# Final norms of a one-core backbone step: one VectorE pass is given to ScalarE and GpSimd, and loads are moved ahead of the last scatter

## The reference

```python
def layer_norm(x, g, b):
    mu = jnp.mean(x, axis=-1, keepdims=True)
    var = jnp.mean(jnp.square(x - mu), axis=-1, keepdims=True)
    return (x - mu) * lax.rsqrt(var + LN_EPS) * g + b
x = layer_norm(DEEPNORM_ALPHA * x1 + g2 * moe(h, p), ln2_g, ln2_b)
```

## Time and profile before

| | us |
|---|---|
| median of three runs | 1805.2 |
| lowest and highest | 1798.62, 1807.9 |
| the profiled execution | 1803.54 |
| its span, first to last instruction | 1801.5 |
| TensorE busy | 1689.4 (94%) |
| VectorE busy | 931.5 (52%) |
| ScalarE busy | 847.2 (47%) |
| GpSimd busy | 768.4 (43%) |

### The profile page before, as it was taken

How to read it: one execution, slowest core, us unless ns; L and a number is a source line. 1 busy time by engine, 2 the same in 40 slices (tenths; PEclk the granted TensorE clock), 3 DMA queues, 4 the chain that set the end, 5 groups by cost and what they waited for, 6 DMA issues and landing times.

```text
span 1801.5 us, 32620 instructions
## 1 busy us (share of the span) xinstructions
PE 1689.4 (94%) x8585; PEld 1319.0 (73%) x8586; DVE 931.5 (52%) x1453; ACT 847.2 (47%) x950; POOL 768.4 (43%) x445
## 2 busy tenths in 40 slices
PE   6999999999899898999999999999999999999944
PEld 2677778888455586888888788788888887878821
DVE  7532311158478883444546465554554655555528
ACT  2321012262032442546667666665756666767612
POOL 2230000400003564437556656566556565665620
PEclk9999999999999898999999999999999999999968
DMA  8515531021552363668978888888879888988776
GB/s 349 176 50 175 176 118 38 24 97 41 216 200 81 118 223 131 239 181 263 307 242 302 293 271 279 281 290 293 266 244 296 265 277 288 284 297 274 231 243 259
DMA packets 102448, 390.77 MB, mean 217 GB/s; under 512 B 21668, under 2 KB 38305, under 8 KB 74625
## 3 DMA queue, kind: packets, MB, share of 16 engines
q1 hardware_dynamic: 62576, 289.25, 43.4%
q0 software_dynamic: 37232, 91.44, 20.0%
q10 hardware_dynamic: 2592, 9.44, 1.7%
HBM read 339.94 MB, written 84.72 MB: 236 GB/s over the span
## 4 chain that ended last, share of the span: by engine, by line
PE 75%; DMA 8%; DVE 7%; ACT 3%; issue 3%; POOL 2%; ACTq 1%; SPq 1%; DVEq 0%; POOLq 0%
PE ps L874 42%; PE ps L2037 12%; PE ps L929 5%; DMA arena<-hx_dram,arena 4%; PE ps L2178 4%; PE ps L1960 2%; PE ps L906 1%; POOL d_split L612 1%; DMA acc_dram<-arena 1%; PE ps L2168 1%; PE ps L2010 1%; DMA arena<-ada_halves 1%; PE ps L1906 1%; PE ps L2072 1%; ACT const L697 1%
## 5 line engine op out<-in xcount | busy, mean ns | idle before, releaser
L874 PE MATMUL ps<-gu_split,xT 128*128 (+1 forms) x2712 | 635.8, 390 | 0.0
L874 PEld LDWEIGHTS ps<-gu_split,xT 128*128 128x128 f32 x2712 | 508.8, 188 | 107.5 <-issue 2.3
L612 POOL TENSOR_TENSOR d_split<-raw,d_split (+1 forms) x65 | 299.7, 4610 | 160.3 <-ACT d_split L676 159.6
L874 PE MATMUL ps<-d_split,hTe 128*128 (+1 forms) x1356 | 345.4, 404 | 15.6 <-ACT arena L752 14.2
L1010 DVE TENSOR_TENSOR gu_split<-raw,gu_split (+1 forms) x130 | 293.5, 2299 | 98.0 <-ACT gu_split L671 98.0
L874 PEld LDWEIGHTS ps<-d_split,hTe 128*128 128x128 f32 x1356 | 250.1, 191 | 69.4 <-issue 19.2
L671 ACT ACTIVATE gu_split<-raw (+1 forms) x130 | 241.9, 1909 | 27.8 <-SPq L510 19.6
L640 POOL DMA_INDIRECT acc_dram<-arena x104 | 168.9, 1624 | 131.2 <-DVE arena L1185 109.0
L631 POOL DMA_INDIRECT arena<-hx_dram,arena x108 | 147.8, 1368 | 143.4 <-DVE arena L1180 114.4
L1174 DVE TENSOR_TENSOR arena<-ps,arena 128x256 f32<-128x256 f32 x113 | 70.3, 622 | 259.0 <-ACT arena L758 258.9
L1164 DVE TENSOR_TENSOR xT<-ps,xT 128x1024 fp32r<-128x1024 f32 x115 | 140.7, 1224 | 107.0 <-ACT xT L730 107.0
(11 more groups left out here) (303 smaller groups left out, 1430.3 us busy)
## 6 DMA issues: line engine op xcount, KB each, us to landing
raw<-w_exp_gate SPq DMA_DIRECT2D x64, 1024.0 KB, 7.1
raw<-w_exp_up SPq DMA_DIRECT2D x64, 1024.0 KB, 11.1
raw<-w_exp_down SPq DMA_DIRECT2D x64, 1024.0 KB, 7.7
arena<-w_ada SPq DMA_DIRECT2D x16, 1024.0 KB, 5.0
arena<-x_dram SPq DMA_DIRECT2D x18, 512.0 KB, 10.7
arena<-acc_dram SPq DMA_DIRECT2D x18, 512.0 KB, 11.3
arena<-ada_halves SPq DMA_DIRECT2D x4, 2048.0 KB, 24.6
w_raw<-w_in SPq DMA_DIRECT2D x16, 512.0 KB, 5.0
```

The lines of the kernel that those rows point to most:

```text
L612: tt(d_split(q, 1), raw_d(q), d_split(q, 0).bitcast(F32), ALU.subtract).then_inc(d_low, 1)
L874: last = mm(dst, lhs(a, j), rhs(b, j), start=(t == 0), stop=(t == len(terms) - 1))
```

## The change

VectorE's fourth pass (L1302) is kept for tile 8 alone. For tiles 0 to 7 VectorE only makes the reciprocal; ScalarE multiplies `acc1_t[i]` in place by it (a Copy with a scale per partition), after the Square and Sqrt of the next tile, and GpSimd adds `ln2_b` and writes `acc_t[i]`. SyncE writes tiles out in order as before, tile 8 after tile 7.

The loads are regrouped. x1 of tiles 3 to 8 is loaded as soon as all experts are split. GpSimd now waits for accumulator 1 first and signals, then for accumulator 0, and signals again; after the first signal `g2_row[1]` and all nine tiles of accumulator 1 are loaded, after the second the nine tiles of accumulator 0. GpSimd also waits, before either, for a count of `xT_ready` that says that the buffer `xT`, which `acc1_t` overlaps, is written no more. Three semaphores of the routing tables (`end_mm`, `cmp_ready`, `blk_mm`) are folded into `rank_mm` and `nb_ready`; those waits stand where they stood.

```diff
@@ SyncE
             sp.wait_ge(gu_low, NE)
             sp.wait_ge(d_low, NE)
+            for i in range(XE, NT):
+                sp.dma_start(x1_t[i], x1_dram[tile(i), :]).then_inc(fin_in[i], 16)
             sp.wait_ge(moe_done, 1)
+            sp.dma_start(g2_row[1], mod_dram[1, 3 * D:4 * D].partition_broadcast(P)).then_inc(fin_in[ST], 16)
+            for i in range(NT):
+                sp.dma_start(acc1_t[:, i, :], acc_dram[1][tile(i), :]).then_inc(fin_in[i], 16)
+            sp.wait_ge(moe_done, 2)
             for i in range(NT):
                 sp.dma_start(acc_t[:, i, :], acc_dram[0][tile(i), :]).then_inc(fin_in[i], 16)
-                sp.dma_start(acc1_t[:, i, :], acc_dram[1][tile(i), :]).then_inc(fin_in[i], 16)
-                if i >= XE:
-                    sp.dma_start(x1_t[i], x1_dram[tile(i), :]).then_inc(fin_in[i], 16)
-            sp.dma_start(g2_row[1], mod_dram[1, 3 * D:4 * D].partition_broadcast(P)).then_inc(fin_in[ST], 16)
             for i in range(NT):
-                sp.wait_ge(fin_ready, i + 1)
+                if i < NT - 1:
+                    sp.wait_ge(fin_ready, i + 1)
+                else:
+                    sp.wait_ge(last_ready, 1)
@@ GpSimd, after the last scatter
-            for p in range(2):
+            pool.wait_ge(xT_ready, NT + last + 4)
+            for p in (1, 0):
                 pool.wait_ge(y_out[p], 8 * last + 32)
-            pool.nop().then_inc(moe_done, 1)
+                pool.nop().then_inc(moe_done, 1)
+            pool.wait_ge(row_ready, 16 * (8 + 3))
+            for i in range(NT - 1):
+                pool.wait_ge(scaled, i + 1)
+                tt(acc_t[:, i, :], acc1_t[:, i, :], ln2_row[:, 1, :], ALU.add).then_inc(fin_ready, 1)
@@ ScalarE
             for i in range(NT):
                 ln_std(2 * NT + i, acc_t[:, i, :])
+                if i:
+                    r = i - 1
+                    act.wait_ge(scale_ready, r + 1)
+                    a(acc1_t[:, r, :], acc1_t[:, r, :], ACT.Copy, scale=lrec[:, r % 2:r % 2 + 1]).then_inc(scaled, 1)
@@ VectorE
                 i = s - 1
-                if i >= 0:
+                if 0 <= i < NT - 1:
+                    r = i % 2
+                    dve.wait_ge(std_ready, 2 * NT + i + 1)
+                    if i >= 2:
+                        dve.wait_ge(scaled, i - 1)
+                    dve.reciprocal(lrec[:, r:r + 1], lstd[:, r:r + 1]).then_inc(scale_ready, 1)
+                elif i == NT - 1:
+                    dve.wait_ge(scaled, NT - 2)
                     scale = ln_scale(2 * NT + i)
-                    stt(acc_t[:, i, :], acc1_t[:, i, :], scale, ln2_row[:, 1, :], ALU.mult, ALU.add).then_inc(fin_ready, 1)
+                    stt(acc_t[:, i, :], acc1_t[:, i, :], scale, ln2_row[:, 1, :], ALU.mult, ALU.add).then_inc(last_ready, 1)
@@ TensorE and VectorE, routing tables
-                    mm(ps[0:1, 7, 0:1], cnt, ones[0:E, :], start=True, stop=True).then_inc(end_mm, 1)
+                    mm(ps[0:1, 7, 0:1], cnt, ones[0:E, :], start=True, stop=True).then_inc(rank_mm, 1)
-                    dve.wait_ge(end_mm, 1)
+                    dve.wait_ge(rank_mm, 7)
...
```

More of the change, by code:

```diff
@@ L419, in build @@
         x0r_in, x1_out, h2_out = (x0r_in0, x0r_in1), (x1_out0, x1_out1), (h2_out0, h2_out1)
-        (sel_ready, rank_mm, nb_ready, end_mm, cmp_ready, blk_mm, tables_ready, dest_ready, empty_out, perm_ready) = (sem(n) for n in (
-             "sel_ready", "rank_mm", "nb_ready", "end_mm", "cmp_ready", "blk_mm", "tables_ready", "dest_ready",
+        (sel_ready, rank_mm, nb_ready, tables_ready, scale_ready, scaled, last_ready, dest_ready, empty_out, perm_ready) = (sem(n) for n in (
+             "sel_ready", "rank_mm", "nb_ready", "tables_ready", "scale_ready", "scaled", "last_ready", "dest_ready",
              "empty_out", "perm_ready"))
@@ L979, in phase3_pe @@
                     mm(ps[0:1, 7, 5 * E:6 * E], C["tokid"][0:E, 0:1], at_pos[:, 0:E], start=True, stop=True)
-                    mm(ps[0:1, 7, 0:1], cnt, ones[0:E, :], start=True, stop=True).then_inc(end_mm, 1)
+                    mm(ps[0:1, 7, 0:1], cnt, ones[0:E, :], start=True, stop=True).then_inc(rank_mm, 1)
                 if b == 6:
-                    pe.wait_ge(cmp_ready, 1)
+                    pe.wait_ge(nb_ready, 2)
                     mm(ps[:, 7, 0:1], cmp_b[:, 0:P], skip, start=True, stop=True)
                     mm(ps[0:NBP - P, 7, 1:2], cmp_b[:, P:NBP], skip, start=True, stop=True)
-                    mm(ps[0:1, 7, 4 * E:4 * E + NBP], ones[0:E, :], cmp_b, start=True, stop=True).then_inc(blk_mm, 1)
+                    mm(ps[0:1, 7, 4 * E:4 * E + NBP], ones[0:E, :], cmp_b, start=True, stop=True).then_inc(rank_mm, 1)
             last = routed_steps(pe, step)
@@ L1264, in phase3_dve @@
                     done(dve.tensor_copy(endc, ps[0:E, 7, 7 * E + 1:7 * E + 2]))
-                    ts(cmp_b, C["blk"][0:E], endc, None, ALU.is_ge).then_inc(cmp_ready, 1)
+                    ts(cmp_b, C["blk"][0:E], endc, None, ALU.is_ge).then_inc(nb_ready, 1)
                 if b == 6:
-                    dve.wait_ge(blk_mm, 1)
+                    dve.wait_ge(rank_mm, 8)
                     for c, n in ((0, P), (1, NBP - P)):
```

## The result

The changed kernel takes 1821.2 us (median of four runs, 1820.0 to 1824.1) against 1805.6 (1798.6 to 1807.9): ratio on record 1.0077, 95% interval 1.0051 to 1.0103, or +14 us with +9 to +19. (The two medians alone give +15.5 us, inside that interval.) Its profiled execution took 1824.1 us, span 1822.0, against 1803.5 and 1801.5.

What follows compares the result with a forecast made beforehand. The end was taken to be set by the start of the first tile's sums and VectorE's 5.43 us per tile. Terms +10.1 - 1.2 - 1.3 + 2.0 + 3.3 = +12.9 us on 1805.2 gave 1818 us, range 1804 to 1825.

Steps and rivals of the forecast that it cites:

- The late start: Loads ahead of tile 0's accumulator in SP's queue delay VectorE's first addition from 1745.06 to 1755.2: +10.1 us.
- the scatters' share: The last two scatters, working beside the regrouped loads, take 4.8 us of all DMA engines before tile 0 can start.
- the completion: Time for the load that tile 0 needs to complete, in the sum for VectorE's first addition: 1 us.
- Tile 1's start: VectorE starts tile 1 at 7.1 us from its first addition, before 8.33: -1.2 us.
- Tile 1's block: VectorE's block for tile 1, free of contention, takes 4.12 us for 5.43: -1.3 us.
- The seven contended blocks: In tiles 2 to 8 GpSimd's addition holds up VectorE's L1298; period 5.72 us for 5.43: +2.0 us.
- The end: After tile 8's block, tile 7's copy, addition and output precede tile 8's output: 8.0 us for 4.7, +3.3.
- The merged semaphores and the wait for xT: Folded routing semaphores order the same instructions; the xT_ready count is full before the last product: 0 us.
- Rival 1: No contention between GpSimd's addition and VectorE's passes; VectorE holds 4.12 us per tile: +1.7 us, 1807; chance 0.18.
- Rival 2: GpSimd and VectorE lock each other out for whole instructions in contended tiles; period 6.29 us: +16.9, 1822; chance 0.17.
- Rival 3: Perfect interleaving: GpSimd's addition slips partly beside L1294, 4.9 us per tile: +7, 1812; chance 0.12.
- Rival 4: Tile 0 is not late: loads fit under the scatters, VectorE starts at 1744, 11.4 us less; chance 0.03.

Runs made afterwards that it cites:

- split only: Changed kernel with the loads put back in the order of the kernel before; ratio to the kernel before 1.0044, stage +7.6 us.
- x in PSUM: Changed kernel with one operand of VectorE's passes over a tile in PSUM, GpSimd's addition unchanged; ratio to the kernel before 1.0041, stage +5.5 us.
- everything: Changed kernel with operands in PSUM, tile 7's fourth pass on VectorE, only two acc1 loads between the scatters' landings; ratio to the kernel before 0.9952.
- tail on VectorE: Changed kernel with tile 7's fourth pass also left on VectorE, GpSimd adding for tiles 0 to 6; ratio to the kernel before 1.0087.

## Why the prediction was right, and where it was off

By its own steps, in the stage:

- **The late start**, +10.1: measured +11.2 (43.6 for 32.4 us). Right in mechanism: seventeen transfers stand in one queue, it does not run dry, and the scatters work beside them. S3 landed some 9 us after its issue (8 was assumed), S4 after 8. The excess of 1.1 us lies in the terms for the scatters' share (4.8 us), the completion (1.0) or the time at which the x1 loads begin (1727.6, read from a window edge); the runs do not part them.
- **Tile 1's start**, -1.2: -1.1. **Tile 1's block**, -1.3: -1.3.
- **The seven contended blocks**, +2.0: +3.1, from 5.87 us for 5.72. The mis-sized term is the loss of the third pass: 1.78 us, forecast 1.6. GpSimd started at 1.34 us of the block, not at 1.6 (the wait from ScalarE to GpSimd is 0.07 us here, not 0.36), which changes nothing as it stands behind L1311 anyway; and it got 0.14 us done beside L1311, where 0.3 was assumed. Both engines hold on to the end of their instruction: rows 6 had shown that for VectorE's loss, but I took from L1639 that the first engine shares. The GpSimd rows beside it, before, allow the other reading:

```profile
99.97 0.74 POOL L1416 TENSOR_TENSOR arena<-arena 128x256 f32<-128x256 f32 x1 [4.71 <-DVE arena L1619]
100.79 1.07 POOL L1417 TENSOR_TENSOR arena<-arena 128x256 f32<-128x256 f32 x1
```

  L1416 was inside first and took 0.74 us. L1417 took 1.07 for its usual 0.74 and ended at 101.86, and the pair of L1639 ended 0.54 us after that, at 102.40. That is what turns by whole instructions give, with a little done while waiting, as in the 3.06 us rows.
- **The end**, +3.3: +5.9. This is the step that failed: a wait that the sum left out. The way of tile 7 through ScalarE and GpSimd cost what was said: the last output landed 7.6 us after tile 8's block, forecast 8.0. The drain behind it was not in the sum; it adds 3.0. It could have been seen: GpSimd's program ended at 1740 before, and its drain row stood there with 6.68 us.
- **The merged semaphores and the wait for xT**, 0: no run has them alone, but the medians leave little for them. In four kernels that carry them (split only, x in PSUM, everything, tail on VectorE) the ratios are +7.9, +7.4, -8.7 and +15.7 us, the stages +7.6, +5.5, -8.4 and +13.8: at most 2 us lie ahead of the stage. The stage's start in single profiled executions, 1711.3 to 1712.6 in three kernels without them and 1712.6 to 1718.5 in seven with them, would suggest more; ten executions don't settle it.

The sum was +12.9 us; the stage has +17.8, the medians +14 to +15.5. That the predicted 1818 us lies only 3 us from 1821.2, where the terms are 5 us short in the stage, is in part luck: in the medians of four some 2 to 4 us of the stage's +17.8 do not appear, and nothing here tells why.

Rival 1 (no contention) falls by the 3.06 us rows. Rival 2 (a lock for the whole instruction) had the right mechanism and a period that was too long, 6.29: it did not allow for the little that the waiting engine gets done (0.14 us for GpSimd, 0.19 for L1313). Rival 3 falls: GpSimd starts anew in each block. Rival 4 falls with the start at 1758.90. The rule of the Trainium skill ("SBUF — State Buffer", section "Who interferes with whom") is borne out: two SBUF inputs against a reading GpSimd instruction contend (3.06 us), one does not (1.28), a GpSimd instruction that only writes does not (1.28), and whoever is inside keeps the other out. The page of the Trainium skill says that the other "fully blocks"; measured, it gets 0.14 to 0.19 us done.

What stays open: why the time ahead of the stage differs by 7 us and more between profiled executions, and with it a few us of the medians (0.9926 is 13.5 us, of which the stage shows 8; the stage of the kernel before on that chip is not known). Why the drain takes 6.7 us was not tried.

## What to carry to other kernels

Before a pass is handed to GpSimd, look at what it will lie beside: count most of its time as VectorE's (here 1.78 of 2.34 us) wherever VectorE then reads two operands in SBUF and GpSimd reads too, or put one of them in PSUM, which here turned the stage's +17.8 us into +5.5 with nothing moved. Loads that were moved into an idle stretch cost 11.2 us here where they came to stand ahead of the one that the next stage waits for, and gained nothing where few did; ask for each queue what the first consumer needs and what is now ahead of it. And if GpSimd takes part in the last steps, it brings its closing drain with it; let it finish early.

## What the runs showed of the hardware that was not expected

- GpSimd's closing drain ends 6.7 us after its last instruction, even after a mere wait (1797.1 to 1803.8), and set the end of the program in the changed kernel (1821.8 of 1822.0), where GpSimd was among the last.
- The holding is by instruction, in both directions: each of GpSimd's halves of an addition (1.25 us with VectorE idle) took 2.25, the first behind L1312, the second behind L1314. In the changed kernel a reading GpSimd instruction of 2.34 us took 3.33.
- GpSimd's writes of 128x1024 (0.95 us) beside VectorE passes with two SBUF operands cost neither of them anything.
